# Turning the memory and the second mixer's input before their norms, with zero products on TensorE ahead of them

## The reference

```
rms_norm(x, g) = x * rsqrt(mean(x*x) + 1e-6) * g
mem_k, mem_v = split(rms_norm(mem, mem_norm) @ w_mem_kv)        # 1024 x 512
# layer 0
q, k, v, qm = split(rms_norm(h, even_norm1) @ even_w_in)
h += concat(neighbourhood_attention(q, k, v, rpb), memory_attention(qm, mem_k, mem_v)) @ even_w_out
h += swiglu(rms_norm(h, even_norm2), ...)                       # 2816 wide
# layer 1
q, k, v, g, zf, zb, qm = split(rms_norm(h, odd_norm1) @ odd_w_in)
gk_f, gk_b = logsigmoid(zf @ w_f + b_f) / 16, logsigmoid(zb @ w_b + b_b) / 16
o = gla(q, k, v, gk_f) + gla_backward(q, k, v, gk_b)            # linear in q, in k and in v
o = o * rsqrt(mean(o*o) + 1e-6) * g_norm * silu(g)
h += concat(o, memory_attention(qm, mem_k, mem_v)) @ odd_w_out
h += top-2-of-8 expert SwiGLU(rms_norm(h, odd_norm2))           # 3584 wide
out = rms_norm(h, final_norm)
```

## Time and profile before

| | us |
|---|---|
| three timed runs | 1445.82, 1448.41, 1448.61; median 1448.41 |
| the profiled execution | 1446.34, span 1444.1, granted clock 0.996 |
| busy: PE, DVE, ACT, POOL | 1408.7, 1156.4, 974.7, 69.7 |
| PE's first weight product | 15.76 |
| first bias products | 37.24 |
| first product of the second mixer's projection | 340.22 |

### The profile page before, as it was taken

How to read it: one execution, slowest core, us unless ns; L and a number is a source line. 1 busy time by engine, 2 the same in 40 slices (tenths; PEclk the granted TensorE clock), 3 DMA queues, 4 the chain that set the end, 5 groups by cost and what they waited for, 6 DMA issues and landing times.

```text
span 1444.1 us, 19732 instructions
## 1 busy us (share of the span) xinstructions
PE 1408.7 (98%) x7228; PEld 1184.3 (82%) x7228; DVE 1156.4 (80%) x1013; ACT 974.7 (67%) x929; POOL 69.7 (5%) x70
## 2 busy tenths in 40 slices
PE   6999999998999999999999999999999999999997
PEld 6997888887977788888888888888888888888885
DVE  5567756664674888988888899889888889888887
ACT  6455645444853577777777777787777777777775
POOL 0000100000010300100000000000010000000000
PEclk9999999999999999999999999999999999999999
DMA  8634455544454899999999999999999999999992
GB/s 263 218 127 146 152 199 203 177 142 133 137 176 150 299 368 387 355 393 393 374 369 394 386 360 393 386 354 396 395 372 375 393 377 368 396 383 357 393 361 74
DMA packets 201942, 435.88 MB, mean 302 GB/s; under 512 B 10959, under 2 KB 41251, under 8 KB 201892
## 3 DMA queue, kind: packets, MB, share of 16 engines
q1 hardware_dynamic: 198836, 424.70, 81.1%
q0 software_dynamic: 3056, 10.50, 2.5%
HBM read 427.30 MB, written 7.88 MB: 301 GB/s over the span
## 4 chain that ended last, share of the span: by engine, by line
PE 93%; DVE 3%; ACT 2%; issue 1%; DMA 1%; POOL 0%; SPq 0%; DVEq 0%; POOLq 0%; ACTq 0%
PE ps L1583 26%; PE ps L1585 26%; PE ps L1584 26%; PE ps L1865 5%; PE ps L1867 3%; PE ps L2142 2%; DVE w_lo L1003 1%; ACT w_hi L547 1%; DMA raw<-mem_kv 1%; PE ps L1708 0%; PE ps L1672 0%; PE ps L2052 0%; PE ps L2164 0%; PE ps L1999 0%; PE ps L1686 0%
## 5 line engine op out<-in xcount | busy, mean ns | idle before, releaser
L1471 DVE TENSOR_TENSOR w_lo<-raw,w_hi 128x2048 fp32r<-128x2048 f32 (+1 forms) x221 | 436.0, 1981 | 57.0 <-ACT w_hi L847 56.7
L847 ACT ACTIVATE w_hi<-raw 128x2048 fp32r<-128x2048 f32 (+1 forms) x221 | 367.4, 1669 | 119.7 <-PE ps L1585 119.7
L1583 PE MATMUL ps<-w_hi,xt_both 128*128 128x512 f32 (+2 forms) x1048 | 405.8, 387 | 3.3 <-DVE xt_both L1364 1.5
L1585 PE MATMUL ps<-w_hi,xt_both 128*128 128x512 f32 (+2 forms) x1048 | 400.0, 382 | 0.0
L1584 PE MATMUL ps<-w_lo,xt_both 128*128 128x512 f32 (+2 forms) x1048 | 399.4, 381 | 0.0
L1471 DVE TENSOR_TENSOR w_lo<-arena,w_hi 128x2048 fp32r<-128x2048 f32 x144 | 294.8, 2052 | 27.0 <-ACT w_hi L847 26.8
L847 ACT ACTIVATE w_hi<-arena 128x2048 fp32r<-128x2048 f32 x144 | 248.8, 1728 | 82.4 <-PE ps L1585 82.4
L1583 PEld LDWEIGHTS ps<-w_hi,xt_both 128*128 128x128 f32 x1048 | 197.0, 188 | 41.1 <-issue 4.7
L1585 PEld LDWEIGHTS ps<-w_hi,xt_both 128*128 128x128 f32 x1048 | 196.9, 188 | 37.4
L1584 PEld LDWEIGHTS ps<-w_lo,xt_both 128*128 128x128 f32 x1048 | 197.2, 188 | 35.0
L1583 PE MATMUL ps<-w_hi,hT_hi 128*128 128x512 f32 x560 | 219.4, 392 | 0.0
(11 more groups left out here) (266 smaller groups left out, 1223.0 us busy)
## 6 DMA issues: line engine op xcount, KB each, us to landing
raw<-exp_gate SPq DMA_DIRECT2D x72, 1024.0 KB, 7.6
raw<-exp_up SPq DMA_DIRECT2D x48, 1024.0 KB, 8.8
arena<-exp_down SPq DMA_DIRECT2D x48, 1024.0 KB, 6.7
arena<-exp_up SPq DMA_DIRECT2D x40, 1024.0 KB, 8.4
raw<-exp_down SPq DMA_DIRECT2D x40, 1024.0 KB, 8.3
arena<-exp_gate SPq DMA_DIRECT2D x24, 1024.0 KB, 8.5
raw<-exp_up SPq DMA_DIRECT2D x32, 512.0 KB, 6.0
raw<-even_gate SPq DMA_DIRECT2D x11, 1024.0 KB, 5.3
```

The source lines that it names most:

```text
L847: ins = act.activation(w_hi[:, n % CUT, at:at + src.shape[1]], src, ACT.Copy)
L1471: ins = dve.tensor_tensor(w_lo[:, n % CUT, cols], src, w_hi[:, n % CUT, cols].bitcast(F32), ALU.subtract)
L1583: pe.matmul(dst, a[0], b[0], start=start, stop=False, skip_group_check=shared)
L1585: return pe.matmul(dst, a[1], b[0], start=False, stop=stop, skip_group_check=shared)
```

## The change

Both parts use that the root of a norm is one number per token, and can be multiplied in after the product.

At the start the memory is transposed as it is loaded. Its square sums, epsilon and roots come after x's (`NORM_STEP` gives each norm its place in the counts). The root goes into `mv` as ACT's scale and into `mkT` as a row that PE spreads over the partitions (`spread_roots0`), ACT copies, and DVE multiplies by; the engines change tiles, ACT takes `mv` and DVE `mkT`. Slots 0 and 1 are cut in four pieces each. PE multiplies zeros 12 times ahead of the gains and 6 times ahead of slot 0. `turn(1)` moves from between the two halves to a place ahead of the last group of the second. ACT and DVE share x's norm.

In the second mixer PE transposes h itself. The root goes into z's copy and `qm1` (by a spread row, `root1_row`), into the silu's scale, into the squares of o and into `sg` (q's part), and squared (`rstd2`) into v (k's part and v's own). Counts of `in1_copied_a` fall by one since the copy of `qm1` moved to DVE.

The diff, cut:

```diff
+NORM_STEP = (1, 0, 2, 3, 4, 5)
...
-            act.wait_ge(mem_in, 16)
-            mean_squares(0, mem_sb, BY_TOKEN)
-            high_to(0)
+            def high_pieces(n):
+
+                act.wait_ge(landed[n], 16)
+                for k in range(4):
+                    cols = slice(512 * k, 512 * (k + 1))
+                    ins = act.activation(w_hi[:, n, cols], raw[:, n, cols], ACT.Copy)
+                    if k < 3:
+                        ins.then_inc(piece_hi, 1)
+                ins.then_inc(hi_ready, 1)
+                cut[0] = n + 1
+
             act.wait_ge(gains_ready, 1)
             turned_high(0)
+            high_pieces(0)
             act.wait_ge(x_in, 16)
             mean_squares(1, h, BY_TOKEN)
-            norm(1, h, range(TT))
+            high_pieces(1)
+            norm(1, h, range(1))
             high_to(2)
             turned_high(1)
+            act.wait_ge(turned, 8)
+            mean_squares(0, mem_sb, BY_TOKEN)
             high_to(3)
+            act.wait_ge(root0_spread, 1)
+            act.activation(root0_row, ps[:, 2, 0:T], ACT.Copy).then_inc(root0_kept, 1)
             act.wait_ge(slot_done, 2)
-            for b in range(2):
-                act.activation(mkT[:, b, :], ps[:, 4 + b, 0:T], ACT.Copy).then_inc(kv_copied_a, 1)
+            for t in range(TT):
+                act.activation(mv[:, t, :], ps[:, 6 + t, 0:256], ACT.Copy, scale=rstd[:, t:t + 1]).then_inc(kv_copied_a, 1)
...
             for q, piece in enumerate(BY_TOKEN):
+                if q == 2:
+                    turned_high(3)
                 act.wait_ge(ff_added, q + 1)
                 mean_squares(3, h, [piece])
-            norm(3, h, range(1))
-            turned_high(3)
...
-            act.activation(qm1.rearrange("p i t -> p (i t)"), ps[:, 5, :], ACT.Copy,
-                           scale=float(HEAD) ** -0.5).then_inc(in1_copied_a, 1)
+            high_to(I_Q + CUT)
+            act.wait_ge(root1_spread, 1)
+            act.activation(root1_row, ps[:, 6, 0:T], ACT.Copy).then_inc(root1_kept, 1)
...
-                act.activation(sg[:, :, 384 * c:384 * (c + 1)], ps[:, 2 * c:2 * c + 2, 0:384],
-                               ACT.Silu).then_inc(in1_copied_a, 1)
+                for t in range(TT):
+                    ins = act.activation(sg[:, t, 384 * c:384 * (c + 1)], ps[:, 2 * c + t, 0:384], ACT.Silu,
+                                         scale=rstd[:, 3 * TT + t:3 * TT + t + 1])
+                ins.then_inc(in1_copied_a, 1)
...
+            dve.memset(hT_hi[:, 0, :].bitcast(F32), 0.0).then_inc(warm_ready, 1)
             dve.wait_ge(gains_turned, 1)
             dve.tensor_copy(gain_of[:], ps[:, 7, 0:5 * KD]).then_inc(gains_ready, 1)
-            add_eps(0, BY_TOKEN)
-            norm(0, mem_sb, range(TT))
-            low_to(0)
+            def low_pieces(n):
+
+                for k in range(4):
+                    cols = slice(512 * k, 512 * (k + 1))
+                    if k < 3:
+                        dve.wait_ge(piece_hi, 3 * n + k + 1)
+                    else:
+                        dve.wait_ge(hi_ready, n + 1)
+                    ins = dve.tensor_tensor(w_lo[:, n, cols], raw[:, n, cols], w_hi[:, n, cols].bitcast(F32), ALU.subtract)
+                    if k < 3:
+                        ins.then_inc(piece_lo, 1)
+                ins.then_inc(lo_ready, 1)
+                cut[0] = n + 1
+
             dve.wait_ge(gains_ready, 1)
-            turned_low(0)
+            turned_low(0, range(2))
+            low_pieces(0)
+            turned_low(0, range(2, 4))
             add_eps(1, BY_TOKEN)
-            low_to(1)
+            low_pieces(1)
+            norm(1, h, range(1, TT))
             low_to(2)
             turned_low(1)
+            add_eps(0, BY_TOKEN)
...
-            dve.tensor_copy(mv[:], ps[:, 6:8, 0:256]).then_inc(kv_copied_v, 1)
+            dve.wait_ge(root0_kept, 1)
+            dve.tensor_tensor(mkT[:], ps[:, 4:6, 0:T], root0_row.unsqueeze(1).broadcast_to([P, 2, T]),
+                              ALU.mult).then_inc(kv_copied_v, 1)
...
+            turned_low(3)
             add_eps(3, BY_TOKEN)
-            norm(3, h, range(1, TT))
-            turned_low(3)
 
             products(I_Z + 1)
-            dve.tensor_copy(zT[0:2 * RANK], ps[0:2 * RANK, 4, 0:T]).then_inc(zT_ready, 1)
+            low_to(I_Q + CUT)
+            dve.wait_ge(root1_kept, 1)
+            dve.tensor_tensor(zT[0:2 * RANK], ps[0:2 * RANK, 4, 0:T], root1_row[0:2 * RANK], ALU.mult).then_inc(zT_ready, 1)
+            dve.scalar_tensor_tensor(qm1, ps[:, 5, :].rearrange("p (i t) -> p i t", i=2), float(HEAD) ** -0.5,
+                                     root1_row.unsqueeze(1).broadcast_to([P, 2, T]), ALU.mult, ALU.mult
+                                     ).then_inc(qm1_ready, 1)
+            dve.wait_ge(rstd_ready, 4 * TT)
+            dve.tensor_tensor(rstd2[:], rstd[:, 3 * TT:4 * TT], rstd[:, 3 * TT:4 * TT], ALU.mult).then_inc(rstd2_ready, 1)
...
+                        if i == 0:
+                            pe.wait_ge(mem_in, 16)
+                        elif k % 4 == 0:
+                            pe.wait_ge(xn_ready[t], (0, 0, 0, 2)[i] + k // 4 + 1)
...
+            def keep_busy(count):
+
+                for _ in range(count):
+                    pe.matmul(ps[:, 4, :], hT_hi[:, 0, 0:P], hT_hi[:, 0, :], start=True, stop=True)
+
+            pe.wait_ge(warm_ready, 1)
+            keep_busy(12)
             pe.wait_ge(early_in, 16)
             pe.wait_ge(gains_in, 16)
             pe.transpose(ps[:, 7, 0:5 * KD], gain_rows, ident[0:5 * KD, 0:5 * KD]).then_inc(gains_turned, 1)
             turn(0)
             kv = ([(ps[:, 4 + i, 0:T], "by feature", all_t, slice(P * i, P * (i + 1))) for i in range(2)]
                   + [(ps[:, 6 + t, 0:256], "by token", tok[t], slice(256, 512)) for t in range(TT)])
-            project(0, kv, fresh=norm_halves(0), halves=range(1), left=memory_of)
+            def memory_products(half):
+
+                w = slot(half, 4)
+                for g, (dst, form, tokens, cols) in enumerate(kv):
+                    if half == 1 and g == len(kv) - 1:
+                        turn(1)
+                    for k4 in range(4):
+                        if g == 0:
+                            if k4 < 3:
+                                pe.wait_ge(piece_lo, 3 * half + k4 + 1)
+                            else:
+                                pe.wait_ge(lo_ready, half + 1)
+                        k = 4 * half + k4
+                        a, b = part(w, k4, cols), memory_of(k, tokens)
+                        if form == "by token":
+                            a, b = b, a
+                        ins = mul3(dst, a, b, k == 0, k == KD - 1)
+                ins.then_inc(slot_done, 1)
+
+            keep_busy(6)
+            pe.wait_ge(xt_lo_ready, 2)
+            memory_products(0)
             pe.wait_ge(xt_lo_ready, 4)
-            turn(1)
-            project(0, kv, halves=range(1, 2), left=memory_of)
+            memory_products(1)
+
+            def spread_roots0():
+
+                pe.wait_ge(rstd_ready, 2 * TT)
+                for t in range(TT):
+                    ins = pe.matmul(ps[:, 2, tok[t]], rstd[:, t:t + 1].broadcast_to([P, P]), ident, start=True, stop=True)
+                ins.then_inc(root0_spread, 1)
...
-            pe.wait_ge(kv_copied_v, 1)
+            pe.wait_ge(xt_lo_ready, 8)
+            spread_roots0()
+            pe.wait_ge(kv_copied_a, 2)
             pe.wait_ge(rp_parts, 7)
             bias_products(0, 2)
...
-            turn(3)
+
+            for t in range(TT):
+                for k in range(KD):
+                    pe.wait_ge(ff_added, 2 * t + k // 4 + 1)
+                    o = T * (k % 2) + P * t
+                    ins = pe.transpose(turn_ps(3, k // 2)[:, o:o + P], h[:, t, P * k:P * (k + 1)], ident)
+                    if t == 1 and k % 2 == 1:
+                        ins.then_inc(turned, 1)
...
+            def spread_roots1():
+
+                pe.wait_ge(rstd_ready, 4 * TT)
+                for t in range(TT):
+                    k = 3 * TT + t
+                    ins = pe.matmul(ps[:, 6, tok[t]], rstd[:, k:k + 1].broadcast_to([P, P]), ident, start=True, stop=True)
+                ins.then_inc(root1_spread, 1)
+
+            by_head(I_Q, 0, before_last=spread_roots1)
             pe.wait_ge(zT_ready, 1)
             pe.wait_ge(zT_ones, 1)
-            pe.wait_ge(in1_copied_a, 1)
+            pe.wait_ge(qm1_ready, 1)
             pe.wait_ge(gate_w_in, 48)
             for i in range(4):
```

More of the change, by code:

```diff
@@ L207, in build @@
         gnb = gain[:, 0:DV]
+        root0_row = gain[:, 768:768 + T]
+        root1_row = gain[:, 512:512 + T]
+        rstd2 = sb("rstd2", [P, TT])
         slot_pair = sb("slot_pair", [P, 2, TT, 2])
@@ L774, in _ @@
             act.wait_ge(slot_done, I_V + 2)
-            act.activation(v1[:, 0, 0:384], ps[:, 0, 0:384], ACT.Copy).then_inc(in1_copied_a, 1)
+            act.wait_ge(rstd2_ready, 1)
```

(29 more changed lines are left out.)

56 lines of the change are left out of this document (30 added, 26 removed).

## The result

| | before | changed |
|---|---|---|
| median of 12 runs | 1448.24 us | 1449.95 us |
| lowest to highest | 1445.24 to 1449.30 | 1445.37 to 1454.31 |
| profiled execution, span | 1446.34, 1444.1 | 1448.07, 1445.9 |

The ratio is 1.0017, with the 95% interval 1.0009 to 1.0025: slower by a little under 0.2%, where the prediction said 1445.2 us, faster. 1449.95 also lies outside the range, which ended at 1449.4. The changed kernel's runs also spread more, over 9 us and not 4.

The account below looks back on a forecast made before the run. The prediction took PE, busy 98% of the span, to bound the kernel. The start's -0.1 and the second mixer's -2.1 gave -2.2 us from a base of 1447.4, so 1445.2 us, with a range of 1441.4 to 1449.4.

Parts of the forecast that it names:

- 36 more at 0.12: At the start, behind the first twelve memory products: 36 further products at 0.12 us each, ending at 20.2.
- rival B: At the start, the clock does not stay up and products run at 0.21: sum +1.0, 1448.4 us, chance 0.15.
- bias products after 38.5: Sign of being wrong: the first relative-position products, forecast near 37.1, start later than 38.5 us.
- about 2.7 us at `rp_parts`: PE's wait for DVE's casts ahead of the bias products, into which the three us won at the start turn.
- The start's -0.1: Forecast gain of the start: bias products at 37.1 against 37.24 before; bounds -1.6 and +1.1 us.
- The chain named (squares, slot 3, casts): Path to the bias products: ACT's turning, square sums, slot 3's high pass, DVE's low pass and casts; 25.8 + 11.3 = 37.1.
- The table load: At the start, ACT's 1.28 us load falls behind `turned`, so ACT turns the memory's block 0 at 9.4, not 8.1.
- The second mixer's -2.1: Second mixer's sum: -2.5 for earlier transposes, +0.25 for spreading products, +0.2 for the silu; bounds -2.5 and 0 us.
- the silu: At the second mixer's gates, two instructions of 0.44 to 0.5 us replace one of 0.82: +0.2 us.
- Rival C: The second mixer gives its gain back, PE waiting at the gates: whole -0.1, 1447.3 us, chance 0.10.
- The rule on pointer operands: At the gates' silu, about 93 ns per ACTIVATE pointer operand; by it two would cost 0.2 us more than one.
- Rival A: The start keeps what it wins, 1.4 to 2.7 us; whole -3.6 to -4.9, 1443.1 us, chance 0.27.

Follow-up runs that it names:

- start alone: The change's start with the second mixer as before, against the kernel before: median 1451.59 us, ratio 1.0027.
- mixer alone: The change's second mixer with the start as before, against the kernel before: median 1445.82 us, ratio 0.9990.
- 24 zeros: The changed kernel with 24 zero products in place of 6 ahead of slot 0: median 1448.72 us, ratio 1.0005 to the kernel before.
- both single edits together: The changed kernel with 24 zero products ahead of slot 0 and the memory's squares ahead of x's blocks: 1446.61 us, ratio 0.9998 to the kernel before.
- 24 and 10 zeros with turn(1) first: Changed kernel, 24 zero products ahead of slot 0, 10 ahead of bias products, turn(1) ahead of memory's second half: 1445.44 us, 0.9989 to the kernel before.
- squares early: The changed kernel with the memory's square sums ahead of x's turned blocks on ACT: 1448.02 us, ratio 1.0007 to the kernel before.

## Why the prediction was wrong

**What failed** is one assumption of the sum: "36 more at 0.12", the step from the first memory product to `turn(1)`. I took the clock to be up there. It fell in the 3.75 us of idle time that my own numbers contained (the granted clock reads 1.00 from 12 to 13 us and 0.50 from 13.5), and 27 products took 0.09 more each, 2.4 us, of which 2.1 reached x's turn. This was rival B, priced at +1.0 and given 0.15. Its mechanism came true: turning x 2.1 later than forecast gave bias products 2.1 later. With zeros up to the first product the forecast's times for x's blocks and for the bias products were met to 0.1 us, so the rest of that sum stood. The kernel before has the same loss, 23 slow products. The forecast took it to be gone because the zeros raise the clock early (they did), and left it to the rival that the wait behind them would lose it again. With that loss left in, the late place of `turn(1)` and of the squares makes the start slower than before, and not equal. The prediction's own sign of being wrong, bias products after 38.5, was there: 39.19.

**The second part of the error** is that B was thought of at one place. The sum said that PE would wait "about 2.7 us at `rp_parts`" (2.2 measured), and counted this wait as time lost and nothing more. It also let the clock fall: 0.6 in the bias products and 1.0 behind them. I had seen PE idle for over 4 us at 333.6 to 340.22 without a fall and took it as evidence against. One profile of one execution does not show that: among the ten profiles here with a wait ahead of z's projection, its products are slow in five (start alone, mixer alone, 24 zeros, both single edits together, and 24 and 10 zeros with turn(1) first) and at full rate in the other five.

**The start's -0.1** is +3.9 us in the timed run of the start alone (interval 2.3 to 5.6). In the changed kernel's profile 1.95 + 0.6 + 1.0 of it can be placed. The chain named (squares, slot 3, casts) was right: it is the chain of the changed kernel (27.88 to 39.19), and with the squares moved the casts no longer held the bias products. **The table load** was on the path, by 1.05 us, and the forecast had it; the trace showed no drain behind it, 8.20 + 1.28 to 9.50.

**The second mixer's -2.1** measured -1.5 (interval -2.9 to -0.1). Its terms: 2.8 for the earlier transposes against 2.5; the spread 0.44 against 0.25, since the two float32 products appear as four instructions of 0.11; the silu 1.05 for two against 0.82 for one, +0.2, as forecast. That sums to -2.1, as forecast, partly by luck, since the first two misses cancel. The slow products behind the gates, 1.5 us in executions that have them, were not in the sum. The gates did not wait. Rival C is out.

**The rule on pointer operands**, which stood beside the sum: the Trainium skill ("ScalarE: Activation LUTs", What ACT_TABLE_LOAD costs) puts about 93 ns on each pointer operand, 0.19 for the two silus. The trace after agrees as far as it goes, with 0.23 more (1.05 against 0.82); no run here has the split without the operand, so it does not tell the two apart.

**Rival A** did not happen: the start kept nothing of what it won. The range's upper end took B at its central price only, though the price was known up to +6.4. Some of the prediction's sums are off by 0.1 (the parts of the path to the casts add up to 11.4, not 11.3, and rival A's start of 1.4 to 2.7 with the mixer's 2.1 to 3.5 to 4.8); nothing hangs on that.

What stays open: the last 0.5 us given back, in the experts and the tail, and 1.2 us of what the zeros are worth. Fewer than 24 zeros, just as many as the wait needs, were not tried, nor was turn(1) in its old place with the clock left down.

## What to carry to other kernels

Where an edit starts PE earlier, ask what it waits for next: the products behind a wait can run at half rate, and that comes on top of the wait (here 2.4 us behind 3.75, and 1.6 behind 2.2). And ask what the forecast's base had: a slow stretch that is there before the change is still there after it unless something in the change takes it away. Filling the waits with products whose result nobody reads was worth about 0.1% each time here, at the edge of what can be told, if they ended by the time the real operand came; too many of them become the path, as they did in two kernels here. A clock that falls in some executions and not in others is judged by many runs, not by one trace. The mean granted clock helps within one kernel; between kernels it can leave out a slow stretch.

## What the runs showed of the hardware

Products of zeros hold the clock: with 24 ahead of slot 0 the granted clock reads 1.00 from 10 to 20 us, and the products there follow each other in 0.12. Behind an idle time of 3.75 us it fell to the 1.2 GHz level in all three profiles here that had this wait (changed, start alone, squares early; in the last one only from the seventh product on). Behind waits of 1.2 to 2.4 us it fell in some and not in others: ahead of z's projection in five of ten, ahead of the bias products in four of six. Where other products filled these waits, or there was none, it did not fall there (four and eight profiles). It also fell with PE fully busy, behind eight products that use 33 of the array's rows (361.65 to 364.42 in the changed kernel); such a fall is in seven of fourteen profiles. The granted clock's row does not show the first slow stretch of an execution: from 14 to 22 us the kernel with the second mixer alone reads

```profile
14.00:22.00 8.00, 6.36 (x31) 1.00 0.88 287
```

while 27 of its products there follow each other in 0.21. Rates have to be read from the products.
